# The input projection as plain full-precision products instead of a rounded part and a remainder

## The reference, cut to what matters

```python
h = rms_norm(x, norm1_g)
z = jnp.einsum('btd,de->bte', h, w_in)     # 520 tokens x 1024, times 1024 x 3336
a_b, a_c, a_h, b_val, b_gate, qkv, c_gate, c_beta, c_alpha = jnp.split(z, offs, axis=-1)
```

## Time and profile before

| | us |
|---|---|
| median of 3 runs | 879.94 |
| lowest and highest | 877.75 and 883.81 |
| span of the profiled execution | 876.5 |
| first product of the input projection (L1636) starts | 34.6 |
| last one ends | 246.0 |

### The profile page before, as it was taken

How to read it: one execution, slowest core, us unless ns; L and a number is a source line. 1 busy time by engine, 2 the same in 40 slices (tenths; PEclk the granted TensorE clock), 3 DMA queues, 4 the chain that set the end, 5 groups by cost and what they waited for, 6 DMA issues and landing times.

```text
span 876.5 us, 12140 instructions
## 1 busy us (share of the span) xinstructions
PE 680.9 (78%) x4468; PEld 493.8 (56%) x4469; DVE 378.6 (43%) x570; ACT 201.0 (23%) x401; POOL 239.2 (27%) x268
## 2 busy tenths in 40 slices
PE   2699978789889999978898840978889766978840
PEld 2699977679778889854344430544444433444410
DVE  3605999997347666546212453112112110111128
ACT  5113325634222341241001110101101110101103
POOL 1527479975230010110000024122122221321210
PEclk9989989889989999995889965899989997999985
DMA  9013322112071000035111541299999975895926
GB/s 278 26 49 98 97 73 71 51 49 54 6 247 65 1 1 1 1 118 198 32 48 49 191 168 28 69 413 408 410 414 405 410 310 213 313 386 222 404 75 246
DMA packets 73209, 146.70 MB, mean 167 GB/s; under 512 B 14568, under 2 KB 50604, under 8 KB 64831
## 3 DMA queue, kind: packets, MB, share of 16 engines
q1 hardware_dynamic: 67327, 137.38, 42.7%
q0 software_dynamic: 5824, 8.54, 2.8%
HBM read 139.65 MB, written 16.60 MB: 178 GB/s over the span
## 4 chain that ended last, share of the span: by engine, by line
PE 51%; DVE 25%; DMA 13%; issue 4%; ACT 4%; POOL 1%; SPq 1%; POOLq 0%; DVEq 0%; ACTq 0%
PE ps L1919 17%; DMA wd<-w_down 8%; PE ps L1709 8%; PE ps L1859 7%; PE ps L1636 7%; DVE yT L1179 6%; DVE acc L1189 4%; DMA xo<-h_rows,otok 1%; DVE XX L1355 1%; PE ps L1880 1%; DVE cv L1197 1%; DVE x L1568 1%; PE ps L1949 1%; PE ps L1619 1%; PE ps L1842 1%
## 5 line engine op out<-in xcount | busy, mean ns | idle before, releaser
L1919 PE MATMUL ps<-gu,xT 128*64 128x256 f32 x1024 | 128.3, 409 | 30.2 <-DMA wd<-w_down 15.0
L1636 PE MATMUL ps<-hhi,whi 128*128 128x256 f32 (+1 forms) x416 | 125.1, 301 | 18.7 <-POOL wlo L927 8.3
L1919 PEld LDWEIGHTS ps<-gu,xT 128*64 128x64 f32 x1024 | 80.6, 148 | 85.5 <-issue 35.4
L1636 PE MATMUL ps<-hhi,wlo 128*128 128x256 f32 (+1 forms) x416 | 122.9, 295 | 0.0
L1636 PE MATMUL ps<-hlo,whi 128*128 128x256 f32 (+1 forms) x416 | 122.7, 295 | 0.0
L1636 PEld LDWEIGHTS ps<-hhi,whi 128*128 128x128 f32 x416 | 84.4, 203 | 24.7 <-POOL wlo L927 15.9
L927 POOL TENSOR_TENSOR wlo<-wraw,whi 128x1024 fp32r<-128x1024 f32 x26 | 77.1, 2971 | 66.5 <-ACT whi L609 66.4
L1636 PEld LDWEIGHTS ps<-hhi,wlo 128*128 128x128 f32 x416 | 84.5, 203 | 0.0
L1636 PEld LDWEIGHTS ps<-hlo,whi 128*128 128x128 f32 x416 | 84.2, 202 | 0.0
L1531 DVE SCALAR_TENSOR_TENSOR gact<-gth,ps 128x128 f32<-128x128 f32 x32 | 9.2, 288 | 148.6 <-ACT gth L891 148.6
L1919 PE MATMUL ps<-wd,aT 128*64 128x512 f32 x256 | 62.0, 605 | 11.7 <-ACT aT L895 11.7
(11 more groups left out here) (360 smaller groups left out, 1062.8 us busy)
## 6 DMA issues: line engine op xcount, KB each, us to landing
gu<-w_gate SPq DMA_DIRECT2D x32, 1024.0 KB
gu<-w_up SPq DMA_DIRECT2D x32, 1024.0 KB
wd<-w_down SPq DMA_DIRECT2D x32, 1024.0 KB
wraw<-w_in SPq DMA_DIRECT2D x26, 512.0 KB
wout<-w_out SPq DMA_DIRECT2D x1, 4096.0 KB, 16.5
yk<-expert_rows SPq DMA_DIRECT2D x8, 512.0 KB, 6.4
x<-x_prompt SPq DMA_DIRECT2D x4, 512.0 KB, 5.7
s<-state_delta SPq DMA_DIRECT2D x4, 512.0 KB, 6.1
```

The source lines that it names most:

```text
L1636: last = mm(ps[:, 2 * (n % 2) + half, 0:hi - lo], weights[:, c, :], h[:, c, lo:hi], start=c == 0 and j == 0, stop=c == KT - 1 and j == len ...
L1919: last = mm(ps[g * CAP:(g + 1) * CAP, bank, 0:width], left(c), right(c, g), start=c == 0, stop=c == steps - 1)
```

## The change

The split goes away. `hhi`, `hlo`, `whi` and `wlo` and their semaphores are removed, and so are the instructions that made them: on ACT 5 roundings of tokens and 26 of weights, on POOL 2 remainders of tokens and 26 of weights, on DVE 3 remainders of tokens. `project(n)` waits for the block's transfer itself and issues one plain float32 product per slice and half, 16 a block, from `wraw` and `hT`. POOL's loop becomes `glu`, then `mix_a` and `save_columns` in the same order. All four `wraw` slots and `hT` move into the region of the projection, and DVE waits once more, for POOL's `raw_saved`, before the delta rule.

```diff
-        hhi = proj("hhi", [P, KT, T], F32R)
-        hlo = proj("hlo", [P, KT, T], F32R)
-        whi = [proj(f"whi{s}", [P, KT, P], F32R) for s in range(WSLOTS)]
-        wraw = [proj("wraw0", [P, KT, P])]
+        hT = proj("hT", [P, KT, T])
+        wraw = [proj(f"wraw{s}", [P, KT, P]) for s in range(WSLOTS)]
...
-        def rest_of_tokens(eng, i):
-
-            eng.wait_ge(h_hi, i + 1)
-            eng.tensor_tensor(hlo[:, :, tokens(i)], hT[:, :, tokens(i)], hhi[:, :, tokens(i)], ALU.subtract).then_inc(h_lo, 1)
...
-            def round_tokens(i):
-                act.wait_ge(hT_ready, i + 1)
-                copy(hhi[:, :, tokens(i)], hT[:, :, tokens(i)], ACT.Copy).then_inc(h_hi, 1)
-
-            def round_weights(n):
-                act.wait_ge(weights_in[n % WSLOTS], 16 * (n // WSLOTS + 1))
-                copy(whi[n % WSLOTS][:, :, :], wraw[n % WSLOTS][:, :, :], ACT.Copy).then_inc(w_hi, 1)
...
-                if n + WSLOTS - 1 < NZ:
-                    round_weights(n + WSLOTS - 1)
...
-            for i in range(2):
-                rest_of_tokens(pool, i)
-
-            def rest_of_weights(n):
-                pool.wait_ge(w_hi, n + 1)
-                s = n % WSLOTS
-                nc.gpsimd.tensor_tensor(wlo[s][:, :, :], wraw[s][:, :, :], whi[s][:, :, :], ALU.subtract).then_inc(w_lo, 1)
...
-            for n in range(NZ):
-                rest_of_weights(n)
-                done = n - WSLOTS + 1
-                if done == ZA - 1:
-                    glu()
-                if 0 <= done - ZQ + 1 < 2 * WA:
-                    mix_a(*divmod(done - ZQ + 1, WA))
-                if 0 <= done - ZQ < CQ:
-                    save_columns(done - ZQ)
+            glu()
+            for n in range(ZQ - 1, ZQ + CQ):
+                if n - ZQ + 1 < 2 * WA:
+                    mix_a(*divmod(n - ZQ + 1, WA))
+                if n >= ZQ:
+                    save_columns(n - ZQ)
...
-            for i in range(2, NT):
-                rest_of_tokens(vec, i)
...
+            vec.wait_ge(raw_saved, 3 + 2 * CQ)
...
-                pe.wait_ge(w_lo, n + 1)
+                pe.wait_ge(weights_in[s], 16 * (n // WSLOTS + 1))
...
-                    if n == 0:
-                        pe.wait_ge(h_lo, NT)
-                    parts = [(weights[s], h) for weights, h in ((whi, hhi), (wlo, hhi), (whi, hlo))]
                     for c in range(KT):
-                        for j, (weights, h) in enumerate(parts):
-                            last = mm(ps[:, 2 * (n % 2) + half, 0:hi - lo], weights[:, c, :], h[:, c, lo:hi],
-                                      start=c == 0 and j == 0, stop=c == KT - 1 and j == len(parts) - 1)
+                        last = mm(ps[:, 2 * (n % 2) + half, 0:hi - lo], wraw[s][:, c, :], hT[:, c, lo:hi], start=c == 0,
+                                  stop=c == KT - 1)
```

More of the change, by code:

```diff
@@ L22 @@
 I32 = mybir.dt.int32
-F32R = mybir.dt.float32r
 AX_X = mybir.AxisListType.X
@@ L183, in build @@
         proj = Region(K1, K2)
-        hhi = proj("hhi", [P, KT, T], F32R)
-        hlo = proj("hlo", [P, KT, T], F32R)
-        whi = [proj(f"whi{s}", [P, KT, P], F32R) for s in range(WSLOTS)]
-        at = [proj.at]
-        wraw = [proj("wraw0", [P, KT, P])]
+        hT = proj("hT", [P, KT, T])
+        wraw = [proj(f"wraw{s}", [P, KT, P]) for s in range(WSLOTS)]
         late = Region(K1, K2)
@@ L194, in build @@
         stb = Region(K5 - 1920, K5)("stb", [P, 2, NS * (WB - 1)])
-        hT = Region(K2, K3)("hT", [P, KT, T])
         convd = Region(K2, K3)
@@ L202, in build @@
         first = Region(K4, K5 - 1920)
-        at += [first.at + n * 4096 for n in range(WSLOTS - 1)]
-        wraw += [first(f"wraw{s}", [P, KT, P]) for s in range(1, WSLOTS)]
-        wlo = [Region(a, a + 4096)(f"wlo{s}", [P, KT, P], F32R) for s, a in enumerate(at)]
         raw = [first(f"raw{s}", [P, RAW]) for s in range(3)]
@@ L333, in build @@
         tiles_in = [16 * len(range(s, NZ, WSLOTS)) for s in range(WSLOTS)]
-        w_hi, w_lo, h_hi, h_lo = sem("w_hi"), sem("w_lo"), sem("h_hi"), sem("h_lo")
         x_squared, rstd_ready = sem("x_squared"), sem("rstd_ready")
@@ L1219, in _ @@
             vec.wait_ge(ba_done, 1)
-            vec.wait_ge(h_lo, NT)
             for n in range(ZQ, NZ + 4):
```

## The result

| | before | after | forecast |
|---|---|---|---|
| median, 20 runs each (us) | 879.99 | 874.98 | 874 |
| ratio, 95% interval | | 0.992, 0.9897 to 0.9943 | 0.993 |
| lowest and highest | 877.25, 884.11 | 865.73, 883.18 | |
| span of the profiled execution | 876.5 | 868.5 | 870.5 |
| products of the projection, first start to last end | 34.6 to 246.0 | 26.1 to 239.7 | 27.4 to 240.0 |

The medians are over all runs, while the ratios and intervals leave out runs in a slower state of the chip: 4 of the 20 of the changed kernel here, and further down 3 of the 6 of mixed_4_again and 3 of the 10 of after_pad.

A forecast was written before the change was run, and what follows sets the result against it. The projection was taken as bound by PE at first, later by waits for DVE, which POOL's subtractions stop. +33.3, -32.6, -7.2 and +0.5 us made span 870.5; plus 3.4, time 874, range 867 to 884.

The forecast's parts named there:

- The last step, from span to time: Whole kernel: the median lies 3.4 us above the profiled span, so span 870.5 gives 874 us.
- The price of a block: Projection on PE: a block of plain products takes 7.02 us, 1.28 more than now, 33.3 us over 26 blocks.
- two passes: Rival, projection: a plain product takes two passes, blocks of about 3.5 us, time near 800; chance 0.02.
- the sum: Projection: start, blocks, PE's other work, clock losses and one short wait put the last block's end at 240.0, against 246.0.
- The start: First projection product at 27.4, 7.2 us earlier, no longer waiting for hlo; 2.1 us of DVE time beside hlo come back.
- The clock's losses: First blocks of the projection: low clock still costs 2.8 us in blocks 0 and 1, 1.4 in blocks 2 and 3.
- The wait for the second inversion: Late projection rounds: PE waits about 0.5 us because the second inversion of norms begins only after round 21's spreading.
- The waits: Projection: 32.6 us of PE waiting for DVE's rounds, and the low clock behind such waits, vanish.
- The balance: Projection stage: +33.3 products, -32.6 waits and their clock, -7.2 start, +0.5 short wait.
- Faster by the clock: Rival, first blocks: both clock losses vanish, gain 10.2 us, time 869.7; chance 0.18, shared with a better start.
- PE pausing in the rounds: Rival, projection rounds: PE waits for DVE's normalization, 6.6 us each; three more pauses give 894; chance 0.17.
- Weight loads showing: Rival, projection products: weight loads come on top of each record, 98 us more, time 972; chance 0.01.

The follow-up runs named there:

- mixed_4_again: mixed_products_4 measured once more, unchanged: 866.96 us, ratio 0.9745 to the kernel before.
- after_pad: The changed kernel with 64 register moves that do no work ahead of PE's first wait: 872.37 us, ratio 0.9878 to the kernel before.
- pool_sub_out_2: The kernel before without POOL's remainder of the weights; the product that used it reads whi and hlo a second time: 844.54 us, ratio 0.961.
- pool_sub_back: The changed kernel with a POOL subtraction per block put back, its result read by nothing: 877.76 us, ratio 0.9989 to the kernel before.
- token_split_back: The changed kernel with the tokens' rounding and remainders put back and the first product waiting for them: 879.17 us, ratio 0.9987 to the kernel before.
- mixed_products_4: The changed kernel with only blocks 0 to 3 plain, blocks 4 to 25 split, their remainders on DVE: 866.70 us, ratio 0.9879 to the kernel before.
- its copy with moves: mixed_products_4 with 64 register moves that do no work ahead of PE's first wait: 865.06 us, ratio 0.9793 to the kernel before.
- mixed_products: The changed kernel with blocks 0 to 9 plain, blocks 10 to 25 split, their remainders on DVE: 862.05 us, ratio 0.9817 to the kernel before.

## Why the prediction was right

The time was forecast at 874 and came out at 874.98; more to the point, the steps came out, with errors that nearly cancelled.

**The last step, from span to time, was right by luck.** The forecast added 3.4 us to a span of 870.5. The profiled span is 868.5, 2.0 less, and the median lies 6.5 above it. Every execution took some 1.7 us longer than its own span (the profiled one of the changed kernel 870.22 for 868.5); the rest is where the profiled execution fell among the others, 4.8 us below the median for the changed kernel and 1.8 below it for the kernel before, by the same 1.7. With single runs from 865.7 to 883.2 us, an agreement of 1 us in the whole time shows little; the end of the stage, 239.7 against 240.0, shows more.

**The price of a block** (7.02): right, 7.02 between evacuations. Records stand 0.22 us apart, as in the earlier trace rows. At two passes, as I read the Trainium skill, Perfetto Trace Analysis, Engine Utilization, blocks would by estimate stand some 3.5 us apart; the evacuations above refute that reading and agree with the four passes of the Trainium skill, FP8 and Floating Point Precision, TensorE Precision Notes. Taken for each record, of which a plain product has two, the halved rate fits: by estimate 0.217 us for 260 columns, against 0.219 measured.

**What the sum left out.** Behind a small group of products a block takes 7.21 in the chain, not 7.02. With 12 such blocks the sum was short by 2.3 us. The old trace had shown it: the last block in the earlier trace rows took 5.95, not 5.74. **The start** was 26.1, not 27.4: the 2.1 us that POOL's `hlo` had cost DVE came back as forecast, and PE's transposes of parameters took 1.7 us instead of 2.8 as well. Why is not shown, as the profile grants the full clock there in both traces. **The clock's losses** came to 1.7 and 1.6, not 2.8 and 1.4. **The wait for the second inversion** was 0.09 us, not 0.5. Together: 240.0 + 2.3 - 1.3 - 0.9 - 0.4 = 239.7, as measured; that it fits to the tenth is chance, since differences of 0.1 or 0.2 us are left out.

**The waits.** Forecast: 32.6 us of waits and low clock vanish because DVE is no longer stopped by POOL. In the changed kernel PE has no wait in the rounds. For the old block's price the run without the subtraction shows the cause (pool_sub_out_2), and also that the 32.6 us were not all of it: 26.8 went. The 5.8 that stayed are the price of changing groups (some 2.3), the one wait (1.4) and lower clock. So the forecast had the changes of group vanish with the waits, and they came back as the 2.3 above. That the subtraction acts through DVE is read from DVE's busy time and the chain, as said with that run. For the changed kernel's own price it was named incompletely: pool_sub_back shows that plain blocks are slow enough for DVE to keep up even with the subtractions. Two things each suffice there, the missing subtraction and the longer block; the prediction named the first and left the second to a remark. DVE had even more room than forecast, 18.7 us ahead of block 10 where the prediction's times leave 9: its 34 taps ended at 99.3, not 109.3.

**The start's cause** was half right. I put the 7.2 us down to the wait for `hlo` and to `hlo`'s hold on DVE. The experiments divide it: 4.1 us are the split of the tokens (token_split_back), and some 4.4 more were the subtractions of weights that ran beside DVE's remainders. (Alone in the changed kernel they cost 4.1, pool_sub_back.)

**The rivals.** Faster by the clock: it came in part, 0.9 us of 4.2. PE pausing in the rounds: did not occur. Weight loads showing: the loads (0.19 us long) lie under records 0.22 us apart. None gave its time.

**The balance** of +33.3, -32.6, -7.2 and +0.5 explains why so large a change moves so little: it removes a bound on DVE and pays for it with nearly the same amount on PE. Measured, it is +33.3 for the products, -8.5 for the start, and so -31.1 for all the rest, which makes the -6.3 at the end of the stage.

## What to carry to other kernels

Before trading one engine's work for another's, ask whether the work has to be where it is: here the remainder's harm lay in POOL making it beside DVE's work, not in the split product, and keeping it for the later blocks, on DVE, took the kernel 17 us below the one before, where dropping the split everywhere took it 5. Price the new bound from records of the same kind in the same trace, and add the small cost of every change of group. And when a stage gets shorter and the time does not, compare the stages behind it in two profiles before blaming scatter.

## What the runs showed of the hardware that was not expected

- A plain float32 product has the price of four passes over its columns at 2.4 GHz: 0.438 us for 260 columns (four passes by estimate 0.433), 0.87 for 512 (0.853), in two records, with the loads of weights (0.19 us) hidden.
- A POOL subtraction of 128x1024 beside DVE's taps stretches one tap from 0.74 us to 2.88 in the old trace. Five of them fell into the 34 taps of the old trace (36.2 us instead of 22.6, with other work of POOL beside the last ones), four shorter ones into those of pool_sub_back (29.2), where DVE had time to spare. It also reached the scaling of tokens, which has one tensor as input (1.34 to 2.75). The Trainium skill, SBUF — State Buffer, "SBUF: two separate sides", describes the pair of ports that VectorE and GpSimd share as an exclusive lock, taken by DVE for operations with two SBUF inputs or in a 2-port mode; the stretched taps agree, and which mode the scaling ran in no run here shows.
- In the expert stage PE stands for 3 to 5 us at several points without a wait that the profile shows, while the transfers are near their full rate (a share of 0.99 during the hole at 543.7 to 548.9 in mixed_products_4). The points were the same in both profiles of mixed_products_4 and in its copy with moves, but not in the two of mixed_products. The stage took 8 to 11 us more in kernels that differ from mixed_products only far ahead of it. Why is not known.
